# Joint scores of the last 16 query rows of two heads, and one latent-query product per pair of heads

## The reference, cut to what matters

```
q      = (cq @ w_q_up)            # per head 64 "nope" + 32 rotary columns, 528 + 32 tokens
q_lat  = q_nope @ w_uk[head].T    # 256 wide, the decode's 32 tokens alone use it here
s      = (q . k) * scale, causal  # prompt: 528 x 528 per head
p      = softmax(s)               # row maximum, exp, sum, normalise
o      = p @ v                    # 64 wide per head
```

## Time and profile before

| what | us |
|---|---|
| median of 3 runs (1436.04 to 1438.38) | 1437.58 |
| the profiled execution, its own time | 1435.41 |
| its span in the trace | 1433.6 |
| stage of the heads in it, 92.66 to 284.23 | 191.6 |

### The profile page before, as it was taken

One profiled execution on the slowest core, in us unless ns is written; L12 is line 12 of the kernel. 1 busy time (PEld: TensorE's weight loads), 2 busy tenths in 40 slices (PEclk: granted clock), 3 DMA queues, 4 the chain that ended last, 5 costly groups with the idle time before them and its releaser, 6 DMA issues.

```text
span 1433.6 us, 26921 instructions
## 1 busy us (share of the span) xinstructions
PE 1403.7 (98%) x10451; PEld 1295.5 (90%) x10451; DVE 650.5 (45%) x971; ACT 526.1 (37%) x856; POOL 230.7 (16%) x317
## 2 busy tenths in 40 slices
PE   9989999899999999999999999999999999999997
PEld 9846666556899999999999999999999999999996
DVE  4546666533374333323332578876633332333235
ACT  3235555532243222112221459864422211222234
POOL 0020101000154000000000433655600000000033
PEclk9999999999999999999999999999999999999998
DMA  8221010023223223232223123222322322223301
GB/s 216 64 89 28 20 27 20 4 90 117 74 75 88 81 91 108 59 87 82 80 96 114 34 67 100 62 88 66 106 75 83 121 72 83 69 82 99 122 1 63
DMA packets 180837, 111.15 MB, mean 78 GB/s; under 512 B 25896, under 2 KB 179069, under 8 KB 180768
## 3 DMA queue, kind: packets, MB, share of 16 engines
q1 hardware_dynamic: 180176, 109.41, 26.3%
q0 software_dynamic: 592, 0.79, 0.2%
HBM read 107.15 MB, written 3.02 MB: 77 GB/s over the span
## 4 chain that ended last, share of the span: by engine, by line
PE 86%; DVE 6%; ACT 3%; issue 2%; POOL 1%; SPq 0%; DMA 0%; DVEq 0%; POOLq 0%; ACTq 0%
PE ps L518 52%; PE ps L547 6%; PE ps L794 3%; PE ps L610 3%; PE ps L808 3%; PE ps L1136 2%; PE ps L828 2%; DVE wl L1541 1%; PE ps L811 1%; PE ps L972 1%; PE ps L689 1%; PE ps L785 1%; PE ps L927 1%; PE ps L994 1%; PE ps L682 1%
## 5 line engine op out<-in xcount | busy, mean ns | idle before, releaser
L518 PE MATMUL ps<-xh,wl 128*128 128x280 f32 x1472 | 310.5, 292 | 0.0
L518 PE MATMUL ps<-xh,wh 128*128 128x280 f32 x1472 | 308.8, 291 | 0.7 <-ACT sg L1451 0.7
L518 PE MATMUL ps<-xl,wh 128*128 128x280 f32 x1472 | 307.8, 290 | 0.0
L1541 DVE TENSOR_TENSOR wl<-raw,wh 128x2048 fp32r<-128x2048 f32 (+2 forms) x79 | 196.4, 2486 | 93.0 <-ACT wh L1201 93.0
L1201 ACT ACTIVATE wh<-raw 128x2048 fp32r<-128x2048 f32 (+2 forms) x79 | 162.9, 2062 | 204.9 <-PE ps L518 179.3
L518 PEld LDWEIGHTS ps<-xh,wh 128*128 128x128 f32 x1472 | 233.8, 188 | 1.3 <-ACT sg L1451 1.1
L518 PEld LDWEIGHTS ps<-xh,wl 128*128 128x128 f32 x1472 | 234.6, 189 | 0.0
L518 PEld LDWEIGHTS ps<-xl,wh 128*128 128x128 f32 x1472 | 232.1, 188 | 0.0
L1880 DVE TENSOR_TENSOR ht<-sg,ps 128x560 f32<-128x560 f32 x44 | 32.5, 738 | 269.0 <-PE ps L518 264.8
L2070 POOL TENSOR_TENSOR acc<-xT 128x560 f32<-128x560 f32 x4 | 5.6, 1399 | 753.6 <-DVE xT L1767 648.5
L1453 ACT ACTIVATE hh<-ht 128x560 f32 (+1 forms) x44 | 29.6, 672 | 262.1 <-DVE ht L1880 262.1
(11 more groups left out here) (345 smaller groups left out, 2542.7 us busy)
## 6 DMA issues: line engine op xcount, KB each, us to landing
raw<-in_ffn_w_gu SPq DMA_DIRECT2D x176, 256.0 KB, 3.6
raw<-in_ffn_w_down SPq DMA_DIRECT2D x48, 384.0 KB, 4.3
raw<-in_lru_w_in SPq DMA_DIRECT2D x16, 512.0 KB, 4.5
Ctok<-in_cache_latent SPq DMA_DIRECT2D x48, 128.0 KB, 2.2
raw<-in_mla_w_o SPq DMA_DIRECT2D x16, 256.0 KB, 4.0
raw<-in_ffn_w_down SPq DMA_DIRECT2D x16, 256.0 KB, 5.1
raw<-in_lru_w_o SPq DMA_DIRECT2D x16, 256.0 KB, 3.2
wq<-in_mla_w_q_up SPq DMA_DIRECT2D x16, 144.0 KB, 2.3
```

Of the source, the lines that this page charges most:

```text
L518: mm = pe.matmul(ps[:, 1024 * jp + 512 * h:1024 * jp + 512 * h + TH], w[:, k, col:col + P], x[:, k, h * TH:(h + 1) * TH], start=(k == 0 an ...
L1541: dve.tensor_tensor(wl[u][:, 0:w], raw[u][:, 0:w], wh[u][:, 0:w].bitcast(F32), ALU.subtract).then_inc(lo_ok, 1)
```

## The change

There are two edits, which share the new order of the heads.

First, block 4 of the two heads of a pair is done once, in the head with `u = 1`, ahead of its other blocks. The two products of 16 queries write PSUM partitions 0 to 15 and 64 to 79; maximum, exp, reciprocal, multiplication and the five transposes then run once over 80 partitions. The query projection Q0 stands right behind it in the PE stream. The turns of head `(p, 0)` go into head `(p, 1)` and those of `(p, 1)` into the next pair's first head, four of them; `PT` gets 16 more columns so that both heads find their part of block 4.

Second, the latent queries are one product of two instructions for a pair: `wukT` is one tile of 128 partitions, and a new tile `Qs` of 128 x 64 holds the decode queries of the two heads as diagonal blocks. POOL zeroes it once, and ACT fills a block in each `read_q` with an instruction of its own.

The order of PE with `u = 0` becomes S0 T(p-1,1,0) WT S1 T1 S2 T2 S3 T3 Q0 Q1 out; with `u = 1` it becomes S4(both) T(p,0,0) Q0 S0 T1 S1 T2 S2 T4(both) ql(both) S3 T3 keys Q1 out. `read_k` moves on ACT and DVE to the end of the head. The core of the diff:

```diff
-                for i in range(5):
-                    scores(h, u, i)
-                    if not first:
-                        turn(h - 1, v, i)
+                for n, i in enumerate(range(4) if u == 0 else (4, 0, 1, 2, 3)):
+                    scores(p, u, i)
+                    if u == 1:
+                        turn(p, *((0, 0), (0, 1), (0, 2), (1, 4), (0, 3))[n])
+                    elif not first:
+                        turn(p - 1, 1, i)
...
-                    if i == 1 and u == 1 and not last:
+                    if i == 4 and not last:
                         queries(h + 1, v, 0)
-                    if i == 2:
+                    if i == 2 and u == 1:
                         pe.wait_ge(wt_rd, p + 1)
                         for k in range(KC):
-                            mm = pe.matmul(ps[:, 512 + NS * k:512 + NS * (k + 1)], wukT[u][:, k * P:(k + 1) * P],
-                                           Q[u][0:NOPE, NP:T], start=True, stop=True)
+                            mm = pe.matmul(ps[:, 512 + 2 * NS * k:512 + 2 * NS * (k + 1)], wukT[:, k * P:(k + 1) * P],
+                                           Qs[:], start=True, stop=True)
...
-            def scores(h, u, i):
+            def scores(p, u, i):
-                if above_zero(h * 5 + (0, 0, 1, 2, 4)[i]):
-                    pe.wait_ge(sc_exp, h * 5 + (0, 0, 1, 2, 4)[i])
+                free = p * 9 + ((-1, 0, 1, 2)[i] if u == 0 else 4 if i == 4 else (5, 5, 6, 7)[i])
+                if above_zero(free):
+                    pe.wait_ge(sc_exp, free)
-                    pe.matmul(ps[0:n, 1024:1536], q, K[u][:, 0:512], start=True, stop=True)
-                    pe.matmul(ps[0:n, 1536:1536 + n], q, K[u][:, 512:NP], start=True, stop=False)
-                    mm = pe.matmul(ps[0:n, 1536:1536 + n], identb[0:n, 0:n], maskb[0:n, 0:n], start=False, stop=True)
+                    for s in range(2):
+                        pe.matmul(ps[64 * s:64 * s + META, 1024:1536], Q[s][:, 512:NP], K[s][:, 0:512],
+                                  start=True, stop=True)
+                    for s in range(2):
+                        pe.matmul(ps[64 * s:64 * s + META, 1536:1536 + META], Q[s][:, 512:NP], K[s][:, 512:NP],
+                                  start=True, stop=False)
+                    for s in range(2):
+                        mm = pe.matmul(ps[64 * s:64 * s + META, 1536:1536 + META], identb[0:META, 0:META],
+                                       maskb[0:META, 0:META], start=False, stop=True)
...
+                act.activation(halves(Q[u][0:NOPE, :]), pair(0, 0, 64), ACT.Copy, scale=SCALE)
+                if above_zero(h - u):
+                    act.wait_ge(ql_sum, p)
+                act.activation(Qs[64 * u:64 * u + NOPE, NS * u:NS * u + NS], ps[0:NOPE, 512 + TH - NS:512 + TH],
+                               ACT.Copy, scale=SCALE).then_inc(q_act, 1)
...
-                for i in range(5):
-                    top_score(h, i)
-                    if i == 4 and u == 1 and not last:
-                        read_k(p + 1)
-                    if i >= 1:
-                        normalise(h, u, i - 1)
+                order = (0, 1, 2, 3) if u == 0 else (4, 0, 1, 2, 3)
+                for n, i in enumerate(order):
+                    top_score(p, u, i)
+                    if n >= 1:
+                        normalise(p, u, order[n - 1])
...
-            for u in range(2):
-                dve.memset(Pr[u][:, PR_AT[4]:PR_AT[5]], 0.0)
...
             pool.wait_ge(s_kp2, 2)
+            pool.memset(Qs[:], 0.0).then_inc(d_new, 1)
```

More of the change, by code:

```diff
@@ L50 @@
 SUMS = (0, 5, 10, 14)
+BOTH = 64 + META
 NEG = -1.0e30
@@ L183, in trunk @@
         qrot = put("qrot", [P, B, HEADS, TS])
-        wukT = [put(f"wukT{s}", [NOPE, KV_R]) for s in range(2)]
-        mx = put("mx", [P, 2])
-        rsum = put("rsum", [P, 4])
+        wukT = put("wukT", [P, KV_R])
+        Qs = put("Qs", [P, 2 * NS])
+        mx = put("mx", [P, 3])
+        rsum = put("rsum", [P, 6])
         Ctok = [put(f"Ctok{s}", [P, PAGES, KV_R]) for s in range(2)]
@@ L205, in trunk @@
         V = put("V", [P, 5, HEADS * VH])
-        Pr = [put(f"Pr{s}", [P, PR_AT[5]]) for s in range(2)]
-        PT = put("PT", [P, 4, NP])
-        PT4 = put("PT4", [META, META])
+        Pr = [put(f"Pr{s}", [P, PR_AT[4 + s]]) for s in range(2)]
+        PT = put("PT", [P, 4, NP + META])
+        PT4 = put("PT4", [META, 2 * META])
         put = area(ring_at, ring_at + 4 * W_MAX)
@@ L814, in scores @@
-                mm.then_inc(sc_sum, 1)
[L816 to L829, removed]
+                    w = P * i + P
@@ new lines, in scores @@
+                    pe.matmul(ps[:, bank:bank + w], Q[u][:, P * i:w], K[u][:, 0:w], start=True, stop=False)
+                    mm = pe.matmul(ps[:, bank + P * i:bank + w], identb[:], maskb[:], start=False, stop=True)
+                else:
+                    for s in range(2):
[7 more added lines that the diff above has]
+                                       maskb[0:META, 0:META], start=False, stop=True)
@@ new lines, in scores, with turn @@
+                mm.then_inc(sc_sum, 1)
+            def turn(p, u, i):
+                pe.wait_ge(sc_nrm, scored(p, u, i))
+                free = p * 9 + (2 if i == 4 else ((0, 0, 1, 3)[i] if u == 0 else (4, 5, 6, 7)[i]))
+                if above_zero(free):
+                    pe.wait_ge(pt_rd, free)
+                if i < 4:
+                    bank = 512 * (4 + (i + u) % 2) if i < 3 else 2048
+                    for j in range(i + 1):
+                        mm = pe.transpose(ps[:, bank + j * P:bank + j * P + P],
+                                          Pr[u][:, PR_AT[i] + j * P:PR_AT[i] + j * P + P], ident[:])
+                else:
+                    for j in range(5):
+                        kk, at = P if j < 4 else META, PR_AT[4] + j * P
+                        mm = pe.transpose(ps[0:kk, 2560 + BOTH * j:2560 + BOTH * j + BOTH], Pr[1][0:BOTH, at:at + kk],
+                                          ident[0:BOTH, 0:BOTH])
@@ L881, in head @@
                 if not last:
-                    pe.wait_ge(ql_rd, h + 1)
+                    if u == 1:
+                        pe.wait_ge(ql_rd, p + 1)
                     queries(h + 1, v, 1)
@@ L903, in _ @@
             head(HEADS // 2 - 1, 1)
-            for i in range(5):
-                turn(HEADS - 1, 1, i)
+            for i in range(4):
+                turn(HEADS // 2 - 1, 1, i)
             pe.wait_ge(q_rot, HEADS)
             pe.wait_ge(in_att, 64)
-            pe.wait_ge(d_new, 2)
+            pe.wait_ge(d_new, 3)
             pe.matmul(ps[:, 1536:2048], spread[64:P, :], qrot[64:P, :, :, :].rearrange("p b h t -> p (b h t)"),
                       start=True, stop=True).then_inc(d_q, 1)
-            outputs(HEADS - 1, 1)
+            outputs(HEADS // 2 - 1, 1)
             def fill(g, i):
@@ L1259, in _, with exp, read_pt @@
                                    ACT.Copy).then_inc(s_lte, 1)
[L1261 to L1277, removed]
+            def exp(p, u, i):
+                act.wait_ge(sc_max, scored(p, u, i))
+                n, w, m = (P, P * i + P, i % 2) if i < 4 else (BOTH, NP, 2)
+                bank = 512 * (2 + i % 2)
+                act.activation(Pr[u][0:n, PR_AT[i]:PR_AT[i] + w], ps[0:n, bank:bank + w], ACT.Exp, bias=mx[0:n, m:m + 1],
+                               accum_out=rsum[0:n, 2 * m:2 * m + 1]).then_inc(sc_exp, 1)
+            def read_pt(p, u, i):
+                act.wait_ge(pt_sum, turned_at(p, u, i))
+                if i < 4:
+                    bank = 512 * (4 + (i + u) % 2) if i < 3 else 2048
+                    at = META * u + P * i
+                    act.activation(PT[:, 0:i + 1, at:at + P],
+                                   ps[:, bank:bank + P * (i + 1)].rearrange("p (j q) -> p j q", q=P),
+                                   ACT.Copy).then_inc(pt_rd, 1)
+                else:
+                    act.activation(PT[:, :, 512:512 + 2 * META].rearrange("p j (s q) -> p j s q", s=2),
+                                   both(P, 0, 4), ACT.Copy)
+                    act.activation(PT4[:].rearrange("p (j s q) -> p j s q", j=1, s=2), both(META, 4, 1), ACT.Copy).then_inc(pt_rd, 1)
             def read_k(p):
@@ L1282, in read_k, with read_q @@
                                ACT.Copy).then_inc(k_act, 1)
-            def read_q(h, u):
+            def read_q(p, u):
+                h = p * 2 + u
                 act.wait_ge(q_sum, h + 1)
@@ L1299, in head @@
                 last = isinstance(h, int) and h == HEADS - 1
-                for i in range(5):
-                    if i == 4 and u == 1 and not last:
-                        act.wait_ge(sc_sum, h * 5 + 5)
-                        read_k(p + 1)
-                    exp(h, u, i)
-                    if not first:
-                        read_pt(h - 1, i)
+                for n, i in enumerate(range(4) if u == 0 else (4, 0, 1, 2, 3)):
+                    exp(p, u, i)
```

(17 more changed lines are left out.)

91 lines of the change are left out of this document (46 added, 45 removed).

## The result

The changed kernel takes 1412.12 us (median of 4, 1411.83 to 1412.92); the kernel before took 1437.94 us beside it (1436.04 to 1438.38). The ratio is 0.983, 95% interval 0.982 to 0.984. The profiled execution took 1411.8 with a span of 1410.0; against that of before the span is 23.6 us shorter. Run again later, the ratio was 0.982 (0.980 to 0.984).

A forecast was written before the change was run, and what follows sets the result against it. The prediction took TensorE (PE), busy for 98% of the span, as the bound. Its terms, 7 x (-2.32) + 7 x 0.2 - 2.0 - 0.7 + 0.15 = -17.4 us, took 1437.6 to 1420.2 us, range 1415 to 1431.

The forecast's parts named there:

- rival B: Joint S4: the two heads' products don't run side by side, S4 takes 2.0 us; +7.0, 1427.2 us; chance 0.07.
- D: u = 1 head: each block's scores wait for the exp before in their bank; +9, 1446.5 us; chance 0.04.
- E: Whole kernel: PE's saved time is given back elsewhere and nothing changes, 1437 us; chance 0.03.
- the slack: u = 1 head: three places where DVE or ACT finish only 0.3 to 0.6 us before PE arrives.
- the walk: u = 1 head, timed step by step from S4's start: S0 at 3.0, out's end at 12.7 us against 12.55 before.
- rival C: u = 1 head: one small slack is short, 0.6 to 1.2 us wait per pair; +6.3, 1426.5 us; chance 0.13.
- the ends: Outside the loop's heads: first head -2.0 us, last head with tail -0.7, start of the stage +0.15.
- PE intervals: Step listing each PE instruction's length from start to start, such as S4 1.10, T4 0.57, ql 0.56 us.
- the two head sums: Loop heads: u = 0 loses 2.32 us, 11.20 to 8.9; u = 1 gains 0.2, bounds 0 and +0.6.

The follow-up runs named there:

- joint block 4 alone: The changed kernel with the latent queries done per head again (two `wukT` tiles, no `Qs`): 1420.14 us, ratio 0.988.
- Q0 put back: The changed kernel with Q0 of u = 1 heads behind S1 and its turn, not behind joint S4: 1421.03 us, ratio 0.991.
- joint T4 on 128 rows: The changed kernel with joint T4's five transposes on 128 rows in place of 80: 1414.95 us, one run.
- the latent queries alone: The kernel before with one joint ql per pair (`wukT` as one tile, `Qs`), block 4 and head order as before: 1432.44 us, ratio 0.997.
- T4 on 80 rows: The kernel before with T4's five transposes on 80 rows each, in place of 128 and four of 16: 1437.17 us, ratio 0.999.

## Why the prediction was right and wrong

**Right: the bound and the mechanism.** PE's intervals set the stage before and after, and the gain is their sum. Joint S4 cost one head's S4 (1.11 against 1.2 forecast), so rival B falls. What the prediction drew for B from the Trainium skill (TensorE: Matmul & The Clock Gate, Part 3, The mechanism) was my own step: the sentence is about weight loads and doesn't say that the passes of two column halves come one behind the other. Here both heads take all 128 rows and run as one. Taken alone the sentence doesn't hold in this trace either: the weights of the 16-column products, on all rows, were loaded at 121.39 us, while the 512-column passes, on all rows too, ran until the next ones started at 121.82. D and E didn't come.

**Partly wrong: the slack.** The prediction gave the keys and out 0.3 to 0.6 us of slack. `outputs_lo` ended 7.21 us behind S4's start, as walked 0.3 ahead of the 7.55 at which PE was to come. But PE's intervals were shorter than in the walk, so PE was ready at 7.2 and the slack was used up: about 0.14 us of wait in T3 and the keys, and 0.11 before out, which started 0.3 behind the end of `read_k`. That is rival C's mechanism at under a third of its 0.9 us. Three runs in which PE comes later lose the wait at the keys (joint block 4 alone, Q0 put back, joint T4 on 128 rows). A further saving of PE time between S4 and the keys is worth little in this head until DVE's chain is shorter too.

**Right: the ends, but for the first head.** The last head lost 0.81 us (0.7 forecast), and the stage started 0.14 later (0.15 forecast). The last head's waits are those of the walk, 1.36 us before S0 and 2.16 before out.

**Wrong: the size of the terms, all in one direction.** In the profiled executions the forecast was -17.4, measured -23.6, 6.2 us apart. The u = 0 heads gave 2.63, not 2.32 (7 x 0.31 = 2.2). The u = 1 heads gave 0.19 (the first of them 0.4) in place of costing 0.2 (2.9). The first head gave 2.64, not 2.0 (0.6): its sum left out the ql that this head loses too, and the latent queries alone bring the head from 10.08 to 9.57. The rest of the span gave about 0.4.

The step that failed is "PE intervals" and its use in the two head sums: T4 at 0.57 and ql at 0.56 were taken as the price of their work, when much of both was the price of passes with different numbers of rows standing side by side. Per pair, forecast against measured:
- T4. "Joint T4 has the same ten passes ... so 0.57 stays": the trace had five passes, and 0.57 was in good part the price of going from 128 rows to 16. Joint T4 takes 0.36: 0.21 missed. T4 on 80 rows showed it in the kernel before. Alone it would have changed little: with T4 at 0.55 the head is as long, because of the wait at the keys.
- ql. I booked 0.56 out of the u = 0 head, and out went 0.76, with 0.10 on T2 and 0.10 on S3. For the joint one I had 0.5, and it takes 0.43. That is 0.27 missed, shown by the latent queries alone.
- Q1 in the u = 0 head. Its first pass stood behind the 16-row transposes of T4 and took 0.10 more than the others; with Q0 and Q1 in one piece that goes, 0.12 in all.
- S0. It was to start 3.0 us behind S4 and starts at 2.80: joint S4 is 0.09 shorter than walked, and the way back from ACT to PE took 0.05, where I had put up to 0.2. The wait left is 0.10 (Q0 up to S0 takes 1.52 against 1.42 without a wait), 0.25 forecast. 0.20 missed.
- Against these, S0, T1, S1 and T2 take 1.44 in place of 1.3, because T1 and T2 are five transposes of 0.11 and the T0 and T1 of the old head only three; and S2 takes 0.78 in place of 0.7. Together 0.22.
- The walk came to 12.63 us, and I took 12.75 for the head: 0.12 of allowance that wasn't needed.
- S3 T3, keys and Q1 in the u = 1 head came out as forecast, 4.96 in all, by luck: their waits for DVE took the place of changes of rows or columns that were in the old intervals.

Sum: 0.21 + 0.27 + 0.12 + 0.20 - 0.22 + 0.12 = 0.70, the 0.70 us per pair by which the forecast was short.

**The range.** Its lower end, 1415, took every term that I had read as exact. It was widened for waits and not for the intervals themselves, although start-to-start intervals book a neighbour's cost on the wrong instruction. About 2 of the 8 us to the measured median are something else: I subtracted from a median of 1437.6, while the profiled execution of before took 1435.4; before's runs spread over 2 to 7 us, and the changed kernel's eight runs over 1.3.

## What to carry to other kernels

An interval from start to start is the price of an instruction in its neighbourhood: before it is entered in a sum, compare the same instruction behind and ahead of other neighbours. On a PE-bound stream, count changes in the number of rows between neighbours; padding two kinds of short product to 128 rows with zeros was free here and gave 3.1 us. Where a joint step binds two buffers at once, put independent work right behind it: here that place was worth about 8 us. And when PE time goes, walk the slack of the other engines again with the shorter times: 0.3 us of it was used up by the saving itself.

## What the runs showed of the hardware

A change of rows between neighbouring PE instructions cost time each way. The last 128-row transpose before a 64-row product took 0.10 us more than before a 128-row one. Put on 128 rows with twice the columns, that product and its two neighbours took 0.31 less. From 128-row to 16-row transposes it was 0.15, for a 16-row product between 128-row ones 0.16, for a 16-row mask 0.08. A change of weight columns has a price of the same kind: six passes of Q0 take 1.42 us up to S2, with 128 columns, and 1.51 up to S4, with 16. The Trainium skill (TensorEngine Tiling (Array Packing), Key Properties) says that a change of tiling mode drains the engine; these figures fit it, with 80 rows behaving as 128 do, though no run here shows the drain itself.

TensorE's granted clock fell to its lower level for some microseconds in single executions, in places that differ from one to the next: in the head stage (0.59 over 212 to 216 us with Q0 put back, right behind the 1.36 us wait of the S0 at 212.46, while the 1.37 us wait of the pair before had no fall behind it) or at its end (0.53 over 276 to 290 us with T4 on 80 rows, 0.59 over 258 to 270 with joint T4 on 128). The lower level is 1.2 in place of 2.4 GHz; 14 us at a mean of 0.53 cost up to 6.6 us of PE work, by my estimate from these rows, more than the 2.6 us that that edit gave. What lets it fall in one execution and not in the next stays open.
